# Stick-breaking attention in a two-block transformer: query products at two of four step heads, another order of evictions and exponentials

## The reference

```
q = split_heads(u @ attn_w_q[i])                     # 1024 x 1024 weights
z = einsum('bhqd,bhkd->bhqk', qb, kb) * scale        # causal, in blocks of 128 queries
log_beta      = log_sigmoid(z)
log_one_minus = where(causal, log_sigmoid(-z), 0)
log_remain    = cumsum(log_one_minus, axis=3, reverse=True) - log_one_minus
weights       = where(causal, exp(log_beta + log_remain), 0)
o             = einsum('bhqk,bhkd->bhqd', weights, vb)
h = h + o @ attn_w_o[i]
```

## Time and profile before

| | us |
|---|---|
| median of three runs | 2609.86 (2606.67 to 2611.96) |
| profiled execution, its own time | 2606.49 |
| its span, first to last instruction | 2604.8 |
| TensorE busy | 2527.6 |
| VectorE busy | 1063.0 |
| GpSimd busy | 987.2 |
| ScalarE busy | 714.7 |
| mean granted clock of TensorE | 0.989 of full |

### The profile page before, as it was taken

How to read it: one execution, slowest core, us unless ns; L and a number is a source line. 1 busy time by engine, 2 the same in 40 slices (tenths; PEclk the granted TensorE clock), 3 DMA queues, 4 the chain that set the end, 5 groups by cost and what they waited for, 6 DMA issues and landing times.

```text
span 2604.8 us, 30359 instructions
## 1 busy us (share of the span) xinstructions
PE 2527.6 (97%) x11718; PEld 1998.9 (77%) x11718; DVE 1063.0 (41%) x1587; ACT 714.7 (27%) x930; POOL 987.2 (38%) x321
## 2 busy tenths in 40 slices
PE   9998999989999999989999999999999989999998
PEld 7765787667888888658888888888888666888886
DVE  5463715548422315965223110422311666522301
ACT  3333223323222222242222222222222453222221
POOL 3321343213444433124444444444444553444442
PEclk9999999999999999999999999999999989999999
DMA  4321132212222232512222333322224001222222
GB/s 154 113 81 49 65 113 89 81 41 82 90 97 96 81 100 101 139 45 96 97 97 82 100 109 118 133 95 96 85 92 171 33 17 34 96 97 97 82 100 76
DMA packets 42322, 235.84 MB, mean 91 GB/s; under 512 B 5504, under 2 KB 5504, under 8 KB 21888
## 3 DMA queue, kind: packets, MB, share of 16 engines
q1 hardware_dynamic: 42096, 232.60, 25.9%
q10 hardware_dynamic: 144, 2.10, 0.2%
HBM read 222.86 MB, written 6.29 MB: 88 GB/s over the span
## 4 chain that ended last, share of the span: by engine, by line
PE 90%; DVE 6%; ACT 2%; issue 1%; SPq 0%; DMA 0%; POOL 0%; DVEq 0%; ACTq 0%
PE ps L1485 27%; PE ps L1487 27%; PE ps L1486 27%; PE ps L1873 2%; PE ps L1779 1%; PE ps L1741 1%; PE ps L1712 1%; PE ps L1499 1%; PE ps L1748 1%; PE ps L1859 1%; PE ps L1691 1%; PE ps L1886 1%; PE ps L1700 1%; DVE small L1168 1%; DVE score L1162 0%
## 5 line engine op out<-in xcount | busy, mean ns | idle before, releaser
L517 POOL TENSOR_TENSOR w_lo<-raw,w_hi 128x2048 fp32r<-128x2048 f32 (+1 forms) x206 | 874.3, 4244 | 1422.0 <-ACT w_hi L633 1396.9
L1485 PE MATMUL ps<-x_hi,w_hi 128*128 128x512 f32 x2048 | 810.3, 396 | 9.4 <-DVE sb_q L1401 2.8
L1487 PE MATMUL ps<-x_hi,w_lo 128*128 128x512 f32 x2048 | 799.6, 390 | 0.0
L1486 PE MATMUL ps<-x_lo,w_hi 128*128 128x512 f32 x2048 | 798.6, 390 | 0.0
L1485 PEld LDWEIGHTS ps<-x_hi,w_hi 128*128 128x128 f32 x2048 | 385.1, 188 | 109.2 <-issue 24.2
L633 ACT ACTIVATE w_hi<-raw 128x2048 fp32r<-128x2048 f32 (+1 forms) x216 | 377.6, 1748 | 328.6 <-PE ps L1487 325.1
L1487 PEld LDWEIGHTS ps<-x_hi,w_lo 128*128 128x128 f32 x2048 | 384.9, 188 | 81.0
L1486 PEld LDWEIGHTS ps<-x_lo,w_hi 128*128 128x128 f32 x2048 | 385.5, 188 | 75.9
L1046 DVE TENSOR_TENSOR tmp<-ps,rms_b 128x512 f32<-128x512 f32 x88 | 60.9, 692 | 589.2 <-PE ps L1487 578.7
L1487 PE MATMUL ps<-hid_hi,w_lo 128*128 128x512 f32 x704 | 278.4, 395 | 0.0
L1485 PE MATMUL ps<-hid_hi,w_hi 128*128 128x512 f32 x704 | 278.3, 395 | 0.0
(11 more groups left out here) (211 smaller groups left out, 2500.1 us busy)
## 6 DMA issues: line engine op xcount, KB each, us to landing
raw<-in_w_up SPq DMA_DIRECT2D x88, 1024.0 KB, 4.9
raw<-in_w_down SPq DMA_DIRECT2D x64, 704.0 KB, 4.1
raw<-in_w_feat SPq DMA_DIRECT2D x23, 1024.0 KB, 4.9
raw<-in_w_pw SPq DMA_DIRECT2D x12, 1024.0 KB, 5.0
raw<-in_w_tok SPq DMA_DIRECT2D x8, 1024.0 KB, 4.9
raw<-in_w_out SPq DMA_DIRECT2D x8, 1024.0 KB, 4.9
shifted<-conv_in SPq DMA_DIRECT2D x80, 67.5 KB, 2.1
bias<-in_bias_t SPq DMA_DIRECT2D x8, 512.0 KB, 6.1
```

The source lines that it names most:

```text
L517: nc.gpsimd.tensor_tensor(w_lo[:, s, 0:w], raw[:, s, 0:w], w_hi[:, s, 0:w].bitcast(f32), ALU.subtract).then_inc(lo_ready, 1)
L1485: nc.tensor.matmul(out, hi, src_hi, start=start, stop=False, skip_group_check=True)
L1486: nc.tensor.matmul(out, hi, src_lo, start=False, stop=False, skip_group_check=True)
L1487: return nc.tensor.matmul(out, lo, src_hi, start=False, stop=stop, skip_group_check=True)
```

## The change

The query products of a pair's time are taken at two steps of four. Steps 3, 7, 11, 15 and 19 take three products, and steps 4, 8, 12, 16 and 20 take five. In both kinds of step VectorE does softplus and rounding of both units ahead of the absolute values, and the query eviction stands in the second kind, ahead of the absolute values. The eviction of pairs 0 to 3 goes to the head of steps 7, 11, 15 and 19, that of pairs 4 to 6 to the later part of steps 24, 28 and 32, and that of pair 7 to the end. The low part of query chunk 2 goes from step 1 to step 5. On ScalarE the weights of both units stand ahead of the decays in steps 2 and 3 modulo 4, and the high piece goes to the end of its step; its plan changes as well.

```
-Q_SLOTS = 5 * KD // 2
+Q_STEPS = {}
+for _t in range(5):
+    Q_STEPS[4 * _t + 3], Q_STEPS[4 * _t + 4] = 3, KD - 3
+Q_MOVED = {4 * _t + 4: _t + 3 for _t in range(5)}
-SB_HIGHS = {4: 0, 6: 1, 8: 2, 10: 3, 13: 4, 15: 5, 17: 6, 19: 7, 21: 8, 23: 9, 25: 10, 27: 11}
+SB_HIGHS = {5: 0, 8: 1, 9: 2, 12: 3, 13: 4, 16: 5, 17: 6, 20: 7, 21: 8, 24: 9, 25: 10, 28: 11}
 SB_LOWS = {i + 1: n for i, n in SB_HIGHS.items()}
...
         for i in range(slots + 2):                      # ScalarE
-            if i < slots:
-                sb_decay(2 * i)
-                sb_decay(2 * i + 1)
-            if i in SB_HIGHS:
-                sb_high(SB_HIGHS[i])
+            short_arguments = i % ST >= 2
             for e in range(2):
-                if i >= 2:
+                if i >= 2 and short_arguments:
+                    sb_weights(2 * (i - 2) + e)
+            for e in range(2):
+                if i < slots:
+                    sb_decay(2 * i + e)
+            for e in range(2):
+                if i >= 2 and not short_arguments:
                     sb_weights(2 * (i - 2) + e)
                 if i < slots:
                     sb_logs(2 * i + e)
+            if i in SB_HIGHS:
+                sb_high(SB_HIGHS[i])
...
         for i in range(slots + 3):                      # VectorE
+            beside = i in Q_STEPS
+            if beside and i >= 7 and i % ST == 3:
+                sb_output(i // ST - 1)
             if 1 <= i <= slots:
                 sb_softplus(2 * (i - 1))
                 sb_rounds(2 * (i - 1))
+                if beside:
+                    sb_softplus(2 * (i - 1) + 1)
+                    sb_rounds(2 * (i - 1) + 1)
+            if i in Q_MOVED:
+                sb_query(Q_MOVED[i])
             if i < slots:
                 sb_absolute(2 * i)
                 sb_absolute(2 * i + 1)
-            if i % 4 == 3 and i < Q_SLOTS:
-                sb_query(3 + i // 4)
-            if 1 <= i <= slots:
+            if 1 <= i <= slots and not beside:
                 sb_softplus(2 * (i - 1) + 1)
                 sb_rounds(2 * (i - 1) + 1)
-            if i == 1:
+            if i % ST == 0 and i > 20:
+                sb_output(i // ST - 2)
+            if i == 5:
                 dve.wait_ge(lo_ready, first["q"] + 2)
                 low("q", 2)
             if i in SB_LOWS:
                 sb_low(SB_LOWS[i])
-            if i >= 6 and i % 4 == 2:
-                ...                                     # the pair's eviction, now in sb_output(pair)
+        sb_output(SB_PAIRS - 1)
...
+        taken = KD                                      # TensorE
         for i in range(slots + 3):
-            if i < Q_SLOTS:
-                query_products(KD + 2 * i, KD + 2 * i + 2)
+            if i in Q_STEPS:
+                query_products(taken, taken + Q_STEPS[i])
+                taken += Q_STEPS[i]
```

More of the change, by code:

```diff
@@ L1440, in sb_rounds, with sb_output @@
             nc.vector.tensor_copy(soft_hi[:, soft_span(u)], tmp[:, u % 6, 0:n]).then_inc(sb_rounded, 1)
+        def sb_output(pair):
+            src = ps[:, VALUE_BANK[pair], :]
+            dve.wait_ge(sb_values, 8 * (pair + 1))
+            dve.wait_ge(staged, 2 * (pair + 1))
+            then(nc.vector.tensor_copy(o_hi[:, pair, :], src))
+            by_token = "p (t n) -> p t n"
+            then(nc.vector.tensor_tensor(o_lo[:, :, P * pair:P * (pair + 1)], src.rearrange(by_token, t=ST),
+                                         o_hi[:, pair, :].bitcast(f32).rearrange(by_token, t=ST),
+                                         ALU.subtract))
+            nc.vector.memset(scratch, 0.0).then_inc(y_split, 1)
         slots = SB_HEADS * ST // 2
         for i in range(slots + 3):
+            beside = i in Q_STEPS
+            if beside and i >= 7 and i % ST == 3:
+                sb_output(i // ST - 1)
             if 1 <= i <= slots:
```

## The result

The changed kernel takes 2585.78 us, the median of 4 runs (2585.47 to 2586.22), against 2608.27 us of the kernel before (4 runs, 2606.34 to 2611.96): 22.5 us less. The ratio is 0.9912, with a 95% interval of 0.990 to 0.9924. The prediction was 2588 us. In a later set of runs the changed kernel took 2586.84 us against 2608.89.

The account below looks back on a forecast made before the run. TensorE, busy 97%, bounds the kernel; gains come from its idle and low-clock time in the stick-breaking stage. -9.6 - 14.4 = -24.0 us, less 2 for one clock fall: -22 from 2609.9, so 2588 us; range 2581 to 2600.

Parts of the forecast that it names:

- Second half: Stick-breaking stage, steps 20 to 34: 10.4 us idle and 10.0 us low clock go, 6.0 us idle stays: -14.4 us.
- The ring through three engines: Late pairs: scores wait for weights queued on ScalarE behind decays, these behind VectorE's absolute values; waits of 0.84 and 3.14 go.
- The last steps: End of the second half: arguments and values of the last pair take 5.7 us plus 1.0 for last values, 6.7.
- the cost of the low clock: Second half: 10.0 of TensorE's 54.63 busy us come from the lower clock.
- the walk through VectorE and ScalarE: Late pairs' remaining chain: 6.37 us to step 2's second soft part, then 8.9 to its weights; waits of 0.5 and 1.1.
- First half: Stick-breaking stage, steps 0 to 20: 8.9 us idle goes, 1.4 wait comes, fewer switches save 2.1: -9.6 us.
- "nothing" on the path: Query chunk 2's low part, moved to step 5, lies beside TensorE's work and costs nothing; bounds 0 to 2.3 us.
- cost nothing: First half: eviction (1.3 us), softplus parts and query eviction on VectorE are covered by 2.3 and 3.7 us of query products.
- Rival A: Late pairs: new short waits keep the clock low, so only 14.0 us of idle is won: 2596 us; 16%.
- D: Early pairs: without query products in steps 1 and 2 the clock falls there too, up to 2630 us; 4%.
- B: Late ring no shorter, since moved eviction, low piece and staging delay it; only the first half won: 2600 us; 11%.
- C: Layer behind the stage starts earlier and waits for its weights, so no change: 2610 us; 5%.

Follow-up runs that it names:

- act_order: Kernel before, with ScalarE doing both units' weights ahead of the decays in steps 2 and 3 modulo 4: 2603.56 us, ratio 0.998.
- evict_high: Kernel before, with evictions of pairs 4 to 6 at steps 24, 28, 32 and high pieces later, at their step's end: 2602.86 us.
- late_both: Kernel before, with weights ahead of decays in steps 2 and 3 modulo 4 and the later evictions and high pieces; query products as before: 2591.40 us.
- evict_old: Changed kernel, with the evictions of pairs 4 to 6 back in steps 22, 26 and 30: 2593.22 us, ratio 0.9942.
- high_old: Changed kernel, with the high piece again between ScalarE's decays and its logs, on the changed plan of steps: 2591.68 us.
- low_at_1: Changed kernel, with the low part of query chunk 2 back at step 1 instead of step 5: 2588.32 us.
- weights_first_0: Changed kernel, with weights ahead of decays in step 0 modulo 4 as well: 2585.17 us, ratio 0.9916.
- first_at_2: Changed kernel, with its first three query products at step 2 instead of step 3: 2585.74 us, ratio 0.9918.
- both_better: Changed kernel, with the first three query products at step 2 and weights ahead of decays in step 0 modulo 4 too: 2581.23 us.
- queries_only: Changed kernel, with order of decays and weights, high pieces and evictions of pairs 4 to 6 as before the change: 2600.82 us.

## Why the prediction was right, and where its steps were off

The direction, the size (-22 forecast, -22.5 measured) and the place were right; no rival decided. That the size fits to half a us is in part luck. The stage alone became 20.2 us shorter in the first profile, with one fall of the clock, and 23.0 in the second, without; and errors of some 2 us in the terms cancelled.

*Second half*: -14.4 forecast, -14.8 measured. The ring through three engines was the cause: act_order and evict_high each take waits out of it, late_both takes both, and evict_old and high_old bring waits back from the other side (no run undoes the exponentials' order alone in the changed kernel). The forecast of its length was 44.6 + 6.0 = 50.6 us, and it is 50.26, but three terms were off. A late pair was put at 12.64 + 2.0 = 14.64 us; it takes 14.08, from 2123.41 to 2137.49, the first one 13.22. The last steps were put at 6.7 us without a wait. Their two waits of 0.98 and 0.42 us for the last soft parts are in the measured idle of 3.7; the kernel before has them too (0.97 and 0.40), and the prediction had counted them among the 10.4 us that go. And the cost of the low clock was put at 10.0 us by counting 44.6 us of work at full clock; the changed kernel shows 46.6 busy at 1.00, so it was 8.0. Why the waits are 0.20 + 0.24 + 0.40 and not 2.0: the walk through VectorE and ScalarE was nearly right (6.37 forecast; 6.55 from 2133.16, where the absolute values of step 26 begin, to the end of the second soft part at 2139.71; 8.9 forecast, 8.7 to the scores of step 29 at 2141.83). TensorE's own work beside it was too small: the late step 0 takes 3.70 us without its waits (4.34 between the scores of steps 28 and 29), where 3.10 had been read in the kernel before. Another 0.4 us had been added for collisions, which the measured walk holds already.

*First half*: -9.6 forecast, -5.5 measured in the first profile. Without the fall of the clock it would be -8.3 (88.83 us in the second profile). Right: the first wait (1.4 forecast, 1.13); the switches (three products took 2.27 us, five 3.65, as worked out; TensorE is busy 86.30 us in the second profile, 1.9 less than before, forecast 2.1); the end of the waits before steps 8, 12, 16 and 20. Three terms failed.

The first is the sentence that the low part in step 5 is "nothing" on the path. Beside low_at_1 it costs 0.47 us before the scores of step 9, as shown above. VectorE is busy with it for 2.28 us and comes late to everything up to step 8: the 512-wide absolute values begin 2.57 us behind their scores in step 7 and 2.08 in step 11; in low_at_1 it is 2.09 in both. The timeline of step 5 in the changed kernel:

```profile
2039.76 2.28 DVE L1321 TENSOR_TENSOR w_lo<-raw,w_hi 128x2048 fp32r<-128x2048 f32 x1
2039.93 2.44 POOL L607 TENSOR_TENSOR soft_lo<-tmp,soft_hi 128x128 fp32r<-128x128 f32 x1 [0.97 <-DVE soft_hi L1447]
```

The second is the sentence that the pair's eviction, both softplus parts and the query eviction "cost nothing" beside the query products. A wait of 0.31 us for the weights of step 2 stands before the scores of steps 9, 13 and 17 in low_at_1, and of 0.33 and 0.31 before 13 and 17 in the changed kernel. weights_first_0 ends them all with VectorE's order unchanged, so what makes them is that ScalarE takes the weights behind the narrow decays. That VectorE brings the absolute values for these decays late is seen in the timeline, but no run puts VectorE's order back. Step 8 of the changed kernel, with its second rounding:

```profile
2053.15 1.27 POOL L607 TENSOR_TENSOR soft_lo<-tmp,soft_hi 128x512 fp32r<-128x512 f32 x1 [2.55 <-DVE soft_hi L1447]
2053.70 1.00 DVE L1447 CAST soft_hi<-tmp 128x512 fp32r<-128x512 f32 x1
2054.63 0.68 DVE L1408 SCALAR_TENSOR_TENSOR sb_q<-ps,rms_b 128x512 f32<-128x512 f32 x1
2055.23 0.47 DVE L1431 TENSOR_SCALAR tmp<-ps 128x128 int32<-128x128 int32 x2
```

The scores of step 8 stand at 2053.10, so the absolute values could have begun at about 2053.9; they begin at 2055.23. The rounding takes 1.00 us and not 0.43, since a soft low part runs on GpSimd; it takes as long in step 12 (1.01), where the wait is 0.33, so it isn't what sets step 9 apart. It ends 0.28 us behind the soft low part (2054.42). The Trainium skill (SBUF — State Buffer, Who interferes with whom) says that the one that issues first holds the shared pair and the other is blocked until it is done; the row agrees in that the rounding ended only behind it. The prediction used this rule only for the late pairs, where it would have taken 2 us off the gain. That did not come: the two roundings of step 26 took 0.36 and 0.63 us.

The third is the clock. The prediction took 2 us off for one fall, in the late pairs; it came in the first steps, behind a wait of 1.13 us, and cost 2.7. Rival A's and D's mechanism (a fall behind a short wait, or in an early pair) is thus real, at one place and not in every execution. The rule of the Trainium skill cited for A (TensorE: Matmul & The Clock Gate, A second HAM failure mode) speaks of short idles that come often; this fall came behind a single one. In the late pairs of the changed kernel, with waits of 0.2 to 0.4 us in each, the clock stayed at 1.00 in both profiles.

Rivals B and C: no wait stands behind the moved eviction, and the layer behind the stage has not given the gain back (the two profiles differ by 0.2 us from the last values to the end, 423.65 against 423.45).

What stays open: why the same wait of 1.13 us is followed by a fall in one execution and not in another. Nor was the place of the query products varied beyond the first three, or VectorE's order beside them.

## What to carry to other kernels

Where several engines pass a tile on in order, look for the ring: the operation that frees a buffer may stand, on its engine, behind one that needs the next tile. Put first the one whose input is ready, and clear the ring of all work that nobody waits for; here the stage became 7.1 us shorter by the first move, 9.5 by the second and 15.4 by both. Give independent TensorE work to the steps in which the chain is shortest of time, and check the steps that you take it from: the wait that was covered there can come back elsewhere, as first_at_2 showed, and in both_better it went with its own cause. A piece of work that is moved off one wait may land in front of another four steps later, as the low part did.

## What the runs showed of the hardware that had not been expected

- A wait of 1.13 us in front of narrow products was followed by half clock in one profile of the changed kernel (15.92 us for the first four steps) and not in another (13.21). The variants that keep this wait show all of it: half clock for 6.8 us in high_old and low_at_1, for 3.4 in evict_old and weights_first_0, none in queries_only. A wait of 1.99 us before step 12 was followed by full clock in the kernel before, and by half clock for some 3.4 us in late_both. So one profile can't tell what a short wait costs: here between nothing and 2.7 us more.
- In the late pairs less idle time of TensorE went together with at least nearly as much less busy time, through the clock: 6.7 and 8.0 us in the changed kernel, 3.0 and 5.8 in evict_high, 2.1 and 1.8 in act_order.
- A rounding on VectorE took 1.00 us instead of 0.43 beside a soft low part on GpSimd, and soft low parts stretched beside VectorE's subtraction (in low_at_1 2.9 us for two, of 0.46 each otherwise, beside one of 2.56). So an order of VectorE's work is also an order of GpSimd's.
